# First two modulation items of a GDN / FoX / MoE trunk, handed over by output columns

## The reference, cut to what matters

```
c_act = silu(c)                                  # (1, 1024)
for i in range(2):
    ada = (c_act @ ada_w[i] + ada_b[i])          # (1, 6*1024)
    sh1, sc1, g1, sh2, sc2, g2 = split(ada, 6)
    h = rms_norm(x) * (1.0 + sc1) + sh1          # x is (512, 1024)
    y = mixer(h)                                 # i = 0: gated DeltaNet, i = 1: FoX attention
    x = x + g1 * y
    h = rms_norm(x) * (1.0 + sc2) + sh2
    x = x + g2 * hier_moe(h)
```

## Time and profile before

| | |
|---|---|
| median of 3 runs | 1581.06 us (1574.6 to 4770.37) |
| profiled execution, its time | 1577.59 us |
| its span, first to last instruction | 1575.6 us |
| mean granted TensorE clock | 0.931 |
| PE busy | 1378.9 us (88%) |
| DVE, ACT, POOL busy | 696.4, 476.7, 414.3 us |
| DMA | 351.89 MB, mean 223 GB/s |

### The profile page before, as it was taken

How to read it: one execution, slowest core, us unless ns; L and a number is a source line. 1 busy time by engine, 2 the same in 40 slices (tenths; PEclk the granted TensorE clock), 3 DMA queues, 4 the chain that set the end, 5 groups by cost and what they waited for, 6 DMA issues and landing times. The chain is left out here.

```text
span 1575.6 us, 25794 instructions
## 1 busy us (share of the span) xinstructions
PE 1378.9 (88%) x9261; PEld 924.2 (59%) x9261; DVE 696.4 (44%) x1458; ACT 476.7 (30%) x1081; POOL 414.3 (26%) x609
## 2 busy tenths in 40 slices
PE   4999998989999895999987199999999959999880
PEld 2877777768887553554543187767675445545440
DVE  3655555445655347611111734555556466211114
ACT  3334233244334220111111435555543111111113
POOL 3232022020222002433332333444420023334320
PEclk8799999999999996999999579999999969999996
DMA  8253553543015236999997702221118269999984
GB/s 355 87 201 132 204 194 128 202 151 108 23 54 214 94 114 247 417 423 422 421 422 301 291 15 87 101 80 67 67 67 307 80 244 390 422 423 420 422 361 176
DMA packets 54872, 351.89 MB, mean 223 GB/s; under 512 B 16328, under 2 KB 16800, under 8 KB 29168
## 3 DMA queue, kind: packets, MB, share of 16 engines
q1 hardware_dynamic: 43168, 333.58, 53.2%
q0 software_dynamic: 11520, 16.83, 3.0%
q10 hardware_dynamic: 80, 0.04, 0.0%
HBM read 344.02 MB, written 27.34 MB: 236 GB/s over the span
## 5 line engine op out<-in xcount | busy, mean ns | idle before, releaser
L1205 ACT COPY arena<-PS 128x128 f32<-128x128 f32 (+3 forms) x328 | 154.3, 486 | 519.4 <-PE PS L817 182.0
L734 PE MATMUL PS<-hHi,Whi 128*128 128x512 f32 x512 | 228.4, 446 | 4.7 <-issue 3.8
L736 PE MATMUL PS<-hHi,Wlo 128*128 128x512 f32 x512 | 204.3, 399 | 0.0
L735 PE MATMUL PS<-hLo,Whi 128*128 128x512 f32 x512 | 203.2, 397 | 0.0
L2001 DVE TENSOR_TENSOR arena<-arena,PS 128x128 f32<-128x128 f32 x72 | 20.7, 287 | 340.1 <-ACT arena L1418 273.9
L977 PE MATMUL PS<-Wr,arena 128*64 128x256 f32 x1408 | 166.4, 391 | 3.3 <-DVE arena L1995 3.3
L2189 POOL TENSOR_TENSOR Wlo<-Wr,Whi 128x512 fp32r<-128x512 f32 (+1 forms) x80 | 112.6, 1424 | 200.7 <-ACT Whi L1205 199.7
L977 PEld LDWEIGHTS PS<-Wr,arena 128*64 128x64 f32 x1408 | 102.9, 141 | 79.7 <-issue 31.4
L2244 POOL DMA_INDIRECT y_rows<-arena x72 | 73.9, 1027 | 252.7 <-ACT arena L1205 236.6
L734 PEld LDWEIGHTS PS<-hHi,Whi 128*128 128x128 f32 x512 | 98.5, 192 | 37.0 <-issue 22.5
L736 PEld LDWEIGHTS PS<-hHi,Wlo 128*128 128x128 f32 x512 | 97.8, 191 | 22.5
(11 more groups left out here) (350 smaller groups left out, 2366.7 us busy)
## 6 DMA issues: line engine op xcount, KB each, us to landing
Wr<-in_moe_w_gate_up_dram SPq DMA_DIRECT2D x54, 2048.0 KB
Dr<-in_ada_w_dram SPq DMA_DIRECT2D x42, 1024.0 KB, 26.7
Dr<-in_moe_w_down_dram SPq DMA_DIRECT2D x28, 1024.0 KB
hT<-in_moe_w_down_dram SPq DMA_DIRECT2D x26, 1024.0 KB
arena<-in_moe_w_gate_up_dram SPq DMA_DIRECT2D x12, 2048.0 KB
Wr<-in_gdn_w_dram SPq DMA_DIRECT2D x8, 2048.0 KB, 8.4
Wr<-in_fox_w_dram SPq DMA_DIRECT2D x8, 2048.0 KB, 7.7
shift_scale<-in_moe_w_down_dram SPq DMA_DIRECT2D x12, 1024.0 KB
```

Source lines behind the costliest of these rows:

```text
L734: mm(out_ap, a_hi, b_hi, start=(k == 0), stop=False)
L735: mm(out_ap, a_hi, b_lo, start=False, stop=False)
L736: return mm(out_ap, a_lo, b_hi, start=False, stop=(k == KD - 1))
L1205: return nc.scalar.copy(dst, src)
```

## The change

The weights of items 0 and 1 are laid out by output columns: load a now holds item a mod 2, output columns 256c to 256c+255 with c = a // 2, all eight contraction blocks. So with loads 2c and 2c+1 a quarter c of shift and scale is complete. Partition group j now holds the partial sum over contraction blocks j and 4 + j, and the product that turns rows into columns takes a vector with ones at partitions 0, 32, 64 and 96 (group_heads), one output column, and so also adds the four groups. The bias comes with the small rows (first_bias, with the one already added for the scale), and the two bias loads of the start go. PE runs quarter 0, all four tiles' transposes, columns 0, quarter 1, columns 1, narrow products of blocks 0 and 1, quarter 2, columns 2, narrow 2 and 3, quarter 3, columns 3, narrow 4 and 5, projection of blocks 0 and 1, narrow 6 and 7, the rest of the projection. DVE makes group_heads after its masks, and PE's first quarter waits for it (cols_ok 3). SP's load of item 2 now waits for quarter 3.

```diff
@@ SP
-            sp.wait_ge(consts, 1)
-            for item in range(2):
-                bias_load(item, small_in)
             for a in range(ADA_FIRST):
-                load(first_item(a), ada_w[a // 4, a % 4], ada_first[a // 2])
+                load(first_item(a), ada_w[a % 2, a // 2], ada_first[a // 2])
...
-                        sp.wait_ge(ada_ps, ADA_FIRST)
+                        sp.wait_ge(ada_ps, 3 * 3 + 2)
...
@@ PE
-            pe.wait_ge(small_in, 16 * 4)
+            pe.wait_ge(small_in, 16 * 2)
...
+            def first_quarter(c):
+                pe.wait_ge(ada_first[c], 32)
+                for item in range(2):
+                    for r in range(2):
+                        for j in range(4):
+                            k = 4 * r + j
+                            last = mm((PS[7], PS[0])[item][32 * j:32 * j + 32, ADA_W * (c % 2):ADA_W * (c % 2) + ADA_W],
+                                      cact[:, k:k + 1].to_broadcast([P, 32]), first_item(2 * c + item)[:, k * ADA_W:k * ADA_W + ADA_W],
+                                      start=(r == 0), stop=(r == 1))
+                    last.then_inc(ada_ps, 1)
+            def first_columns(c):
+                pe.wait_ge(first_rows_ok, c + 1)
+                for item in range(2):
+                    for kk in range(2):
+                        at = item * KD + 2 * c + kk
+                        last = mm(PS[1][:, at:at + 1], ada_acc[:, item, kk * P:kk * P + P], group_heads[:], start=True, stop=True)
+                last.then_inc(ada_ps, 1)
+            def write_and_decay(k):
+                pe.wait_ge(h_mod, k + 1)
+                for n in range(NT):
+                    last = mm(PS[6][:, n * 2 * H:(n + 1) * 2 * H], tile(hT[:, k, :], n), abW[:, k, :],
+                              start=(k == 0 and n == 0), stop=(k == KD - 1 and n == NT - 1))
+                last.then_inc(ab_ps, 1)
+            pe.wait_ge(act_setup, 1)
+            pe.wait_ge(cols_ok, 3)
+            for c in range(4):
+                first_quarter(c)
+                if c == 0:
+                    for n in range(NT):
+                        norm_transposes(0, n)
+                first_columns(c)
+                if c > 0:
+                    write_and_decay(2 * c - 2)
+                    write_and_decay(2 * c - 1)
...
-            project(0, 0, 0, KD)
+            project(0, 0, 0, 2)
+            write_and_decay(6)
+            write_and_decay(7)
+            project(0, 0, 2, KD)
@@ DVE
+            link(TS(first_bias[:, 1, :], first_bias[:, 1, :], 1.0, None, ALU.add))
+            nc.vector.tensor_reduce(group_heads[:], ident[:, 0:P:32], AX_X, ALU.add).then_inc(cols_ok, 1)
...
             dve.wait_ge(n_ta, NT)
-            for k in range(KD):
-                TS(hT[:, k, :], hT[:, k, :], modc[:, 1, k:k + 1], modc[:, 0, k:k + 1], ALU.mult, ALU.add).then_inc(h_mod, 1)
+            for c in range(4):
+                dve.wait_ge(ada_ps, 3 * c + 2)
+                cpv(ada_acc[:, 0, :], PS[7][:, ADA_W * (c % 2):ADA_W * (c % 2) + ADA_W])
+                cpv(ada_acc[:, 1, :], PS[0][:, ADA_W * (c % 2):ADA_W * (c % 2) + ADA_W]).then_inc(first_rows_ok, 1)
+                dve.wait_ge(ada_ps, 3 * c + 3)
+                of_c = slice(2 * c, 2 * c + 2)
+                link(TT(modc[:, :, of_c], made[:, :, of_c], first_bias[:, :, of_c], ALU.add))
+                for k in (2 * c, 2 * c + 1):
+                    TS(hT[:, k, :], hT[:, k, :], modc[:, 1, k:k + 1], modc[:, 0, k:k + 1], ALU.mult, ALU.add).then_inc(h_mod, 1)
+                if c > 0:
+                    h_part(0, 2 * c - 2)
+                    h_part(0, 2 * c - 1)
+            h_part(0, 6)
+            h_part(0, 7)
```

More of the change, by code:

```diff
@@ L184, in build @@
         cols = sb("cols", [P, P])
+        first_bias = cols[:, 107:107 + 2 * KD].rearrange("p (i k) -> p i k", i=2)
         cact = sb("cact", [P, KD])
@@ L199, in build @@
         half_m1 = sb("half_m1", [P, 1])
+        group_heads = sb("group_heads", [P, 1])
         ada_acc = sb("ada_acc", [P, 2, ADA_W])
@@ L362, in build @@
         moe_d = sems("moe_d", 2) + [small_in, small2_in, ada_in[1]]
-        moe_d_from = (0, 0, 16 * 4, 16 * 6, 16 * 4 * ADA_HEADS)
+        moe_d_from = (0, 0, 16 * 2, 16 * 6, 16 * 4 * ADA_HEADS)
         n_rs, n_h, n_tr, n_ta, n_tb = sem("n_rs"), sem("n_h"), sem("n_tr"), sem("n_ta"), sem("n_tb")
@@ L470, in ada_loads @@
                     if r % 4 == 0:
-                        if item < 4:
-                            sp.wait_ge(first_rows_ok, 2)
-                        else:
+                        if item >= 4:
                             sp.wait_ge(ada_rowok, item - 3)
@@ L1271, in _ @@
             act.wait_ge(consts, 4)
-            act.wait_ge(small_in, 16 * 4)
+            act.wait_ge(small_in, 16 * 2)
             act.wait_ge(cols_ok, 2)
@@ L1615, in _ @@
             take_tile(0, NT - 1)
[L1617 to L1624, removed]
@@ L1625, in _, with h_part @@
-            dve.wait_ge(n_ta, NT)
-            for k in range(KD):
-                TS(hT[:, k, :], hT[:, k, :], modc[:, 1, k:k + 1], modc[:, 0, k:k + 1], ALU.mult, ALU.add).then_inc(h_mod, 1)
+            def h_part(phase, k):
+                dve.wait_ge(h_hi, phase // 2 * KD + k + 1)
+                if phase == 0:
+                    dve.wait_ge(ab_ps, k + 1)
+                TT(hLo[:, k, :], hT[:, k, :], hHi[:, k, :], ALU.subtract).then_inc(h_lo, 1)
+            made = PS[1][:, 0:2 * KD].rearrange("p (i k) -> p i k", i=2)
@@ L1629, in h_parts @@
+            h_part(0, 6)
+            h_part(0, 7)
             def h_parts(phase):
                 for k in range(KD):
[L1632 to L1635, removed]
+                    h_part(phase, k)
             hn = lambda ap: ap.rearrange("p (h n) -> p n h", h=H)
-            h_parts(0)
             dve.wait_ge(ab_ps, KD)
@@ L2383, in laid_out @@
     rows[104] = a["gdn_norm"][0]
+    rows[107:107 + 2 * KD] = a["ada_b"].reshape(12, KD, P)[0:2].reshape(2 * KD, P)
     rows[105, 0:64], rows[105, 64:] = a["fox_q_norm"][0], a["fox_q_norm"][0]
@@ L2387, in laid_out @@
     g["ada_w"] = a["ada_w"].reshape(2, 4, 2, P, 6, D).transpose(0, 4, 1, 3, 2, 5).reshape(12, 4, P, 2 * D)
+    g["ada_w"][0:2] = a["ada_w"][0].reshape(KD, P, 6, 4, ADA_W).transpose(2, 3, 1, 0, 4)[0:2].reshape(2, 4, P, 2 * D)
     g["ada_b"] = a["ada_b"].reshape(12, 4, ADA_W)
```

## The result

The changed kernel took 1585.43 us in the median of 11 runs, against 1575.85 for the kernel before beside it: ratio 1.0071, 95% interval 1.0049 to 1.0092, so 11 us longer (7.7 to 14.5); the two medians lie 9.6 apart. One execution of the kernel before took 4770.37 us, and the ratio leaves it out. The profiled execution of the changed kernel took 1580.49 us (span 1578.7), 5 us under its median, so it shows only a part of the difference; a second profile, further down, took 1583.50.

What follows compares the result with a forecast made beforehand. PE, busy for 88% of the span, was taken as the bound. The low-clock sum of +9.7 us, less 4.1 for high-clock spells and 0.1 for the start, gave +5.5 on 1577.59: 1583.1 us, range 1575 to 1590.

Steps and rivals of the forecast that it cites:

- the mark: End of the first 24 wide matmuls on PE: 62.39 before, 72.1 at the low clock (+9.7 us), before clock savings.
- Start of quarter 0: First burst on PE waits for group_heads after DVE's masks: start at 17.0 in place of 14.38, 2.6 us later.
- Transposes: All four tiles' transposes on PE follow quarter 0; chain of 8.45 us, last copies end at 29.05.
- Columns: Column passes after each quarter: 1.6 us for eight at the low clock, behind a 0.95 us hand-over of DVE's copies.
- Landing paces nothing: Quarters 2 and 3: weights land at 30.42 and 35.41, long before their turn at about 41 and 50.
- one burst in two: Quarter bursts: half raise the clock for some 3.5 us, 1.5 us saved each, 2.3 for half of three.
- the narrow products of blocks 6 and 7 and the last 18 wide matmuls: End of the stretch before the mark: 3.2 us narrow and 6.7 wide, less 1.3 if the clock is up.
- Rival A: The pieces before the mark hold the clock high: end of wide matmuls at 56.4, -6.0 us, 1571.6; chance 0.13.
- Rival B: No burst before the mark raises the clock, so all of the sum is lost: +9.7 us, 1587.3; chance 0.22.
- Rival C: Later PE waits, as for L1717 (2.3 us), shrink and take up the shift: 1577.6; chance 0.12.
- what lies behind the mark: Later PE work simply begins from the mark; item 2's loads, some 54 in place of 39, cost nothing.
- the rule weighed in the prediction: Transposes before quarter 1 don't count as busy for the clock; by it quarter 1 starts low and +9.7 us comes.

Runs made afterwards that it cites:

- with the bias loads: Changed kernel with the two bias loads back at the start of SP's program, their data unused; ratio 1.0083.
- the 12 matmuls: Twelve unused one-column matmuls at the start of PE, added to the changed kernel (ratio 1.0064) and to the kernel before (ratio 1.0004).
- heads early: Changed kernel with group_heads and the bias addition made before DVE's seven masks; median 1582.62 us, ratio 1.0052.
- filler: Changed kernel with one unused 256-column matmul behind each of bursts 1 to 3; ratio 1.0033.
- the 32 passes: Kernel before with 16 more narrow products (32 passes, unused) ahead of the first wide matmul; ratio 1.0037, 5.8 us.
- by landing: Changed kernel with group_heads early and PE's order written by the landing of the weights; ratio 1.0007.
- before again: Kernel before, unchanged, timed a second time; ratio 0.9996.

## Why the prediction was right, and where its size was off

The forecast was slower by 5.5 us, 1583.1; measured were 1585.4, and 11 us (7.7 to 14.5) by the ratio. The direction, the mechanism up to the mark and the range held; the size was half. That the number itself came within 2.3 us is partly luck: the sum was made on an execution of 1577.59, 1.7 above the median of before that counts, and the changed kernel's median lies 1.6 under what the ratio gives (1575.85 x 1.0071 = 1587.0).

1. Start of quarter 0: forecast 17.0, measured 16.89 and 17.24.
2. Transposes: copies forecast to end at 29.05, measured 28.28 + 0.69 = 28.97.
3. Columns: 1.6 us by my price of 0.20 a pass; measured 1.72 start to start (36.02 to 37.74), 0.22 a pass. Hand-over 0.95: measured 0.9 idle.
4. Landing paces nothing: bursts 2 and 3 at 41.25 and 48.83, without a wait.
5. The mark: forecast 67.9; 67.14 in the first profile and 67.91 in the second, 67.55 with the bias loads, 70.25 with the 12 matmuls: 68.2 on the mean. The kernel before has 62.39, 62.14, and 61.79 with the 12 matmuls, 62.1 on the mean: 6.1 us. The sum was right, and by luck, since two of its parts were off against each other. I had one burst in two raise the clock; in these four profiles it rose behind 3 of 12 (bursts 1 to 3). And I had the narrow products of blocks 6 and 7 and the last 18 wide matmuls take 3.2 + 6.7 us, less 1.3; in three of the profiles they took 1.7 + 4.2, all at the high clock, 4.0 less, and in the fourth 3.3 + 5.5.
6. Rival A's clock, up behind every burst, was seen in single executions (heads early, filler; marks 59.27 and 61.98 where A had 56.4), never in a median. Rival B's price, +9.7, is near the measured loss, but not by its mechanism alone: the marks stayed below 72. Rival C fell by the 32 passes, which were carried to the end (5.8 us of 6.8).

**The term that was mis-sized** is the one that I put at zero: what lies behind the mark. In six profiles with the split by columns (the changed kernel twice, with heads early, by landing, with the filler, with the bias loads) ACT's distance to before grew by 2.4 to 2.8 us between 95 and 108, where PE's wait for head 0's fourth ada load was 2.4 to 2.7 us in place of 1.4 and the next burst ran at 1.93 in place of 1.07. In before again it grew by nothing, with the 32 passes neither. Of the 2.7 us some 1.2 are the longer wait and the rest is the low clock behind it. Mark and this step give 6.1 + 2.7 = 8.8 of the 11, within the interval. That is a ledger of profiles, and the medians don't bear the step out: in three pairs that differ in the fetch (before, 0.9996 and 1.0004; the changed kernel, 1.0065 and 1.0064; the order by landing, 1.0007 and 1.0003, there with fillers too) the time differs by at most 1.3 us, each ratio known to 3 or 4 us. And for the order by landing the ledger says 4.6 - 2.5 = 2.1 us under before, where 1.1 over was measured (-1.7 to 4.1), so 3 us are missing there as well. I had checked that item 2's loads come in time; I had not asked how close the next loads run. That PE's instruction count decides whether the fetch meets the load is shown by the 12 matmuls in the kernel before. Why the same idle time lowers the clock in one kernel (1.93 for the burst behind it) and not in the other (1.07) stays open, and so do the last 2 or 3 us.

On the rule weighed in the prediction: in the changed kernel PE had transposes alone from 20.44 to 28.2, and the clock read 0.82 in 24 to 29 and 0.50 in 29 to 30. The tile at 26.69 took 1.55 in place of 1.09. But with the same transposes in the second profile of this kernel the clock read 1.00 all the way from 24 to 30, and with the filler it fell and came back up while PE still had nothing but transposes, from 20.54 until columns 0 at 30.81. Three rows of that PE timeline, then two windows:

```profile
25.48 1.90 PE L673 MATMUL PS<-ident,arena 128*128 128x128 f32 x8 [2.20 <-DVE arena L1635]
27.57 1.77 PE L673 MATMUL PS<-ident,arena 128*128 128x128 f32 x8 [0.18 <-DVE arena L1635]
30.81 1.05 PE L725 MATMUL PS<-group_heads,ada_acc 128*128 128x1 f32 x8 [1.47 <-DVE ada_acc L1652]
```

```profile
26.00:29.00 3.00, 2.82 (x14) 2.42 (x13) 1.38 (x3) 1.25 (x5) 0.00 (x0) 0.50 1.01 421
29.00:30.00 1.00, 0.34 (x3) 0.10 (x1) 0.62 (x2) 0.62 (x2) 0.00 (x0) 1.00 1.00 418
```

With heads early it went the same way: 0.50 in 23 to 26, 1.00 in 27 to 28, transposes alone since 18.16. By the Trainium skill, page "TensorE: Matmul & The Clock Gate", section "Part 4: PE-mode transpose", transposes don't count as busy. These two traces don't agree: the clock rose from 0.50 to 1.00 behind transposes alone, which ran nearly without a gap (PE busy for 2.82 of 3.00 us).

## What to carry to other kernels

Splitting a serial hand-over into pieces pays only if PE's written order lets it reach each piece when its data lands: here one step put in front (all transposes, behind a wait for a DVE constant) moved every later piece behind its landing, and each piece then added its own hand-over wait and column passes. Put the same pieces in the order of landing before judging the split; and even then, price the idle time that can be filled (6 us here) against the passes that are added (24 x 0.2). A single profile of a stretch in which the clock changes can be 5 us off the typical one: take the marks of several.

## What the runs showed of the hardware

- One instruction fetch of 16 KB (0.98 us on its DMA engine) that fell into a pair of 1 MB loads went with a wait of PE of 2.62 us in place of 1.40 in the kernel before; 48 unused instructions of PE decided whether it did.
- The granted clock rose behind some lone bursts of 3.6 us and not behind others of the same kernel (3 of 12 in four profiles), and a further 256-column matmul behind the burst went with a rise behind each of the three in the profiled execution. Three wide matmuls in each 3 us, with narrow ones between, left it at 0.50. In two traces it rose behind transposes alone.
- Executions of one kernel spread by 21 us (1569.1 to 1590.05, with the filler), and the mean granted clock went from 0.937 to 0.925 with them.
- DVE's scaling of hT (L1655) took up to 1.50 us in place of 0.54 while POOL split the weights, 29.5 to 40. Before, the two never ran together. In the changed kernel it cost nothing, since PE had the burst to do until 35.1:

```profile
29.53 10.44 POOL L2217 TENSOR_TENSOR Wlo<-Wr,Whi 128x512 fp32r<-128x512 f32 x8 [24.52 <-ACT Whi L1224]
...
31.81 1.96 DVE L1655 TENSOR_SCALAR hT<-hT,modc 128x512 f32<-128x512 f32 x2
...
46.81 1.00 DVE L1655 TENSOR_SCALAR hT<-hT,modc 128x512 f32<-128x512 f32 x2
```
